# Nine buffers of prepared weights instead of five in a one-core hybrid decoder layer

## The reference

```python
a = rmsnorm(x, g_mix); u = a @ w_in                     # 1024 x 3080, w_in
# mLSTM heads from q, k, v, gates (chunkwise), short convolution from three more column groups
x = x + jnp.concatenate([h_m, y_c], axis=-1) @ w_out    # 1024 x 1024
f = rmsnorm(x, g_ffn)
x = x + (jax.nn.silu(f @ w_gate) * (f @ w_up)) @ w_down # width 2816
e = rmsnorm(pe @ w_ple, g_ple)                          # pe: 256 wide
x = x + jax.nn.sigmoid(x @ w_pg) * e                    # 1024 x 1024
y = rmsnorm(x, g_final)
```

## Time and profile before

| | |
|---|---|
| median of three runs | 2605.38 us |
| the profiled execution | 2609.61 us, its span 2607.6 us |
| PE busy | 2484.1 us (95%) |
| PEld busy | 2420.1 us (93%) |
| DVE / ACT / POOL busy | 1490.1 / 905.3 / 1014.5 us |
| DMA | 501.02 MB, 192 GB/s |
| granted TensorE clock | 0.983 of full speed |

### The profile page before, as it was taken

How to read it: one execution, slowest core, us unless ns; L and a number is a source line. 1 busy time by engine, 2 the same in 40 slices (tenths; PEclk the granted TensorE clock), 3 DMA queues, 4 the chain that set the end, 5 groups by cost and what they waited for, 6 DMA issues and landing times.

```text
span 2607.6 us, 41062 instructions
## 1 busy us (share of the span) xinstructions
PE 2484.1 (95%) x15829; PEld 2420.1 (93%) x15829; DVE 1490.1 (57%) x2307; ACT 905.3 (35%) x1688; POOL 1014.5 (39%) x785
## 2 busy tenths in 40 slices
PE   8898888999999999999999999999999999999997
PEld 7888778999999998999999999998899999999997
DVE  7667887655555684476643333468357664332355
ACT  5343443343334442334322121354134431211233
POOL 5555655576666242222232122333222232322233
PEclk8999999999999999999999999999999999999999
DMA  6556635576566746575556545575667555564545
GB/s 195 209 174 224 224 133 187 182 274 226 202 227 232 226 148 207 162 243 178 192 169 202 170 148 176 178 231 170 191 181 244 180 187 174 189 211 156 174 140 170
DMA packets 285044, 501.02 MB, mean 192 GB/s; under 512 B 18427, under 2 KB 182612, under 8 KB 284342
## 3 DMA queue, kind: packets, MB, share of 16 engines
q1 hardware_dynamic: 212182, 273.59, 31.1%
q10 hardware_dynamic: 72672, 224.82, 26.4%
HBM read 374.70 MB, written 123.65 MB: 191 GB/s over the span
## 4 chain that ended last, share of the span: by engine, by line
PE 74%; DVE 7%; DMA 3%; issue 3%; POOL 2%; ACT 1%; DVEq 0%; ACTq 0%; POOLq 0%; SPq 0%
PE bank L606 24%; PE bank L608 23%; PE bank L607 23%; DMA wring<-weight_parts 2%; POOL wring L2692 1%; DVE qlo L1798 1%; DMA xs<-x_prompt 1%; PE bank L730 1%; DVE ess L2415 1%; PE bank L797 1%; PE bank L741 1%; DMA wraw<-w_gate 0%; PE bank L719 0%; PE bank L803 0%; DVE wraw L1788 0%
## 5 line engine op out<-in xcount | busy, mean ns | idle before, releaser
L2692 POOL TENSOR_TENSOR wring<-wraw,wring 128x512 fp32r<-128x512 f32 x531 | 775.4, 1468 | 1250.1 <-ACT wring L1295 1247.9
L606 PE MATMUL bank<-qhi,wring 128*128 128x352 f32 (+1 forms) x3588 | 1173.2, 327 | 71.9 <-DVE u L1909 14.5
L608 PE MATMUL bank<-qhi,wring 128*128 128x352 f32 (+1 forms) x3588 | 1157.1, 322 | 0.0
L607 PE MATMUL bank<-qlo,wring 128*128 128x352 f32 (+1 forms) x3588 | 1155.5, 322 | 0.0
L606 PEld LDWEIGHTS bank<-qhi,wring 128*128 128x128 f32 x3588 | 684.0, 191 | 95.3 <-issue 85.1
L607 PEld LDWEIGHTS bank<-qlo,wring 128*128 128x128 f32 x3588 | 683.6, 191 | 0.0
L608 PEld LDWEIGHTS bank<-qhi,wring 128*128 128x128 f32 x3588 | 681.3, 190 | 0.0
L1295 ACT ACTIVATE wring<-wraw 128x512 fp32r<-128x512 f32 x531 | 331.0, 628 | 720.0 <-PE bank L608 549.2
L606 PE MATMUL bank<-hid,wring 128*128 128x352 f32 (+1 forms) x1056 | 340.6, 323 | 13.0 <-DVE wide L2498 7.5
L608 PE MATMUL bank<-hid,wring 128*128 128x352 f32 (+1 forms) x1056 | 339.0, 321 | 0.0
L607 PE MATMUL bank<-hid,wring 128*128 128x352 f32 (+1 forms) x1056 | 338.4, 320 | 0.0
(11 more groups left out here) (317 smaller groups left out, 2361.9 us busy)
## 6 DMA issues: line engine op xcount, KB each, us to landing
wring<-weight_parts ACTq DMA_DIRECT2D x418, 512.0 KB, 4.6
weight_parts<-wring SPq DMA_DIRECT2D x201, 512.0 KB, 4.0
wraw<-w_down SPq DMA_DIRECT2D x33, 1024.0 KB, 6.9
wraw<-w_in SPq DMA_DIRECT2D x14, 1024.0 KB, 6.5
wraw<-w_gate SPq DMA_DIRECT2D x11, 1024.0 KB, 6.0
wraw<-w_up SPq DMA_DIRECT2D x11, 1024.0 KB, 5.9
wraw<-w_in SPq DMA_DIRECT2D x44, 256.0 KB, 5.3
wraw<-w_gate SPq DMA_DIRECT2D x44, 256.0 KB, 4.1
```

What stands on the lines that cost most here:

```text
L606: nc.tensor.matmul(o, hi, mh, start=begins, stop=False, skip_group_check=True)
L607: nc.tensor.matmul(o, hi, ml, start=False, stop=False, skip_group_check=True)
L608: return nc.tensor.matmul(o, lo, mh, start=False, stop=ends, skip_group_check=True)
L2692: nc.gpsimd.tensor_tensor(wlo[e % RING][:, :].rearrange(v, k=k), w.src, whi[e % RING][:, :].rearrange(v, k=k), ALU.subtract).then_inc(lo_d ...
```

## The change

The ring gets nine buffers. The first five stay where they were, the other four lie at the upper end of the core's memory. The room comes from `dynamic_dma_scratch_size=512`: memory that is set aside by default for DMAs issued by POOL is not set aside here, and everything else moves down by as much. The semaphores that count stores and loads of entries are ten of each instead of six.

The start is as before (DVE takes the turns of the first `NEAR` = 5 entries there). In super 0, behind products 49, 56, 63 and 70 of the stage in (the first product of in 7, 8, 9 and 10), each of DVE, ACT and POOL calls `ahead()` once more. From then on ACT and POOL make entry n+8 at product n, DVE the sum of entry n+9, to the end of the program. ACT waits for the entry nine places back.

```diff
-RING = 5
-AHEAD = 4
+PARTS = 10
+RING = 9
+NEAR = 5
+LOOK_FURTHER = (49, 56, 63, 70)
...
-    spare_raw = at("spare_raw", [P, 2048], F32, w0 + 20480 + RING * 4096 + 5632)
+    spare_raw = at("spare_raw", [P, 2048], F32, w0 + 20480 + NEAR * 4096 + 5632)
...
-    wring = [at(f"wring{p}", [P, 1024], F32R, w0 + 20480 + p * 4096) for p in range(RING)]
+    far = nc.sbuf_usable_end // 32 * 32 - (RING - NEAR) * 4096
+    wring = [at(f"wring{p}", [P, 1024], F32R, w0 + 20480 + p * 4096 if p < NEAR else far + (p - NEAR) * 4096)
+             for p in range(RING)]
...
-    mix0 = w0 + 20480 + RING * 4096
+    mix0 = w0 + 20480 + NEAR * 4096
...
-                    before = entries[e - RING].kept
-                    if before:
-                        act.wait_ge(parts_kept[before % 6], 16 * ((before + 5) // 6))
+                    before = entries[e - RING].kept
+                    if before:
+                        act.wait_ge(parts_kept[before % PARTS], 16 * ((before + PARTS - 1) // PARTS))
...
             def in_after(q):
                 def after(s):
+                    if not q.n and s in LOOK_FURTHER:
+                        ahead()
...
-            for e in range(AHEAD + 1):
+            for e in range(NEAR):
                 ahead()
...
-    nc = bacc.Bacc("TRN2", target_bir_lowering=False, num_devices=1)
+    nc = bacc.Bacc("TRN2", target_bir_lowering=False, num_devices=1, dynamic_dma_scratch_size=512)
```

More of the change, by code:

```diff
@@ L287, in build @@
     y_roots = keep("y_roots", [P, 3])
-    assert cursor[0] <= nc.sbuf_usable_end, (cursor[0], nc.sbuf_usable_end)
+    assert cursor[0] <= far, (cursor[0], far)
     y_end = [at(f"y_end{p}", [P, D], F32, R0 + p * 4096) for p in range(3)]
@@ L513, in build @@
         landed = [sem("landed_even"), sem("landed_odd")]
-        parts_kept, parts_loaded = [sem(f"parts_kept{j}") for j in range(6)], [sem(f"parts_loaded{j}") for j in range(6)]
+        parts_kept, parts_loaded = [sem(f"parts_kept{j}") for j in range(PARTS)], [sem(f"parts_loaded{j}") for j in range(PARTS)]
         sums, hi_done, lo_done, prod = sem("sums"), sem("hi_done"), sem("lo_done"), sem("prod")
@@ L595, in entry_ready @@
                 else:
-                    pe.wait_ge(parts_loaded[w.loads % 6], 16 * ((w.loads + 5) // 6))
+                    pe.wait_ge(parts_loaded[w.loads % PARTS], 16 * ((w.loads + PARTS - 1) // PARTS))
             def operand_ready(q, st, i):
@@ L1089, in keep_parts @@
                         sp.dma_start(weight_parts[w.kept - 1], wring[e % RING][:, :].bitcast(F32))\
-                            .then_inc(parts_kept[w.kept % 6], 16)
+                            .then_inc(parts_kept[w.kept % PARTS], 16)
             def spare_weights(i):
@@ L1283, in one_ahead @@
                     if before:
-                        act.wait_ge(parts_kept[before % 6], 16 * ((before + 5) // 6))
+                        act.wait_ge(parts_kept[before % PARTS], 16 * ((before + PARTS - 1) // PARTS))
                 if w.loaded:
-                    act.wait_ge(parts_kept[w.loaded % 6], 16 * ((w.loaded + 5) // 6))
+                    act.wait_ge(parts_kept[w.loaded % PARTS], 16 * ((w.loaded + PARTS - 1) // PARTS))
                     act.dma_start(wring[e % RING][:, :].bitcast(F32), weight_parts[w.loaded - 1])\
-                        .then_inc(parts_loaded[w.loads % 6], 16)
+                        .then_inc(parts_loaded[w.loads % PARTS], 16)
                     return
```

## The result

The changed kernel is slower: 2622.48 us (median of four runs, 2619.66 to 2624.28) against 2605.12 us for the kernel before beside it, a ratio of 1.0065 (95% interval 1.005 to 1.008). A second timing gave 2622.62 against 2606.02 us, 1.0062 (1.0045 to 1.0079). The profiled execution took 2622.72 us, its span is 2620.7 us: 13.1 us more than the span before. The traces so show 13.1 of the 17.4 us between the medians, since the execution profiled before the change lay 4.2 us above its median.

What follows compares the result with a forecast made beforehand. The prediction saw gains only at PE's idle times, mostly waits for DVE's P6 evictions; -6 -4 +0 +1 +1 = -8 took 2609.6 to 2601.6 us profiled, 2597.4 as a median, called 2597.5, range 2585 to 2611.

Steps and rivals of the forecast that it cites:

- (a): Supers 1 and 2: PEld's 8.1 us of waits for loads can go; ends -8.1 and -2, taken as -6 us.
- (b): Gate and up, super 0: sums moved ahead of `hid` and P6 evictions shorten PE's waits; ends -8 and +2, taken -4 us.
- (c): Duo of out, super 0: first raw-load bubble's gain is offset by a second and DVE's longer list; -8 to +5, taken 0.
- (d): In 7 to in 10, super 0: each extra turn costs DVE at most one sum; ends 0 and +5, taken +1 us.
- The exchange named beside it: ACT no longer waits for the store of the entry five back; worth 0 to -3 us to PE, taken with (b).
- (f): Memory, semaphores and SP's list: no instruction added and the memory taken has no user, 0.
- (e): Pg, supers 0 and 1: ACT waits for pg 2's raw load, delaying PE; -1 to +6 per super, +1 together.
- The signs I had named for a wrong forecast: ACT's wait at pg 2 beyond 8 us, or PE's two waits in out together changing by more than 8 us.
- The rule weighed: DVE and POOL exclude each other in SBUF: super 0's sums meet POOL more often, PE +8, 2605.5 us; chance 0.06.
- Slower by the raw load in pg: Rival: ACT stands before a raw load SP can't issue earlier, 6 us in each of two supers, about 2610 us; chance 0.16.

Runs made afterwards that it cites:

- ring_only: The changed kernel with its nine buffers and ten semaphores but no extra turns, splits four entries ahead as in the kernel before: 2594.76 us, ratio 0.9963.

## Why the prediction was wrong

I forecast 2597.5 us, in 2585 to 2611, gave slower 0.16, and measured 2622.48. On the scale of the profiled execution the forecast was 2601.6 and the time is 2622.7 us. By the steps of the prediction, with the change in stall from before to after:

*(a) Waits for loads, supers 1 and 2: -6.* The mechanism was right, the loads' waits went. But supers 1 and 2 without their pg stall 3.2 us less than before, where ring_only, which keeps three waits for loads, has 7.5 us less. The turns bought those waits off and paid more elsewhere, 3.3 us of it in the stage in of super 2 (66.5 us of stall in ring_only, 69.8 after).

*(b) Sums moved in gate and up of super 0: -4, with ends at -8 and +2.* This step failed; it is the one term that came out beyond its ends. Gate 1 gained what I said (3.9 us, and nothing of it in ring_only). Gate 5 gained 4.2 us, but 3.3 of them come with the buffers alone, with S4 still in front of the eviction, so the reason I gave there, that S4 goes, is worth 0.9 us at most. And I took the two places where PE waited before as all that could change, and did not ask where the sums go in the pairs that were free of waits. Behind the up pairs S4, S1 and S2, 4.2 us in the rows above, arrived ahead of the hidden blocks, and the hidden blocks met POOL. Measured: 5.0 us more stall in gate and up than before, 6.6 more than in ring_only.

*(c) The duo of out: 0, with +5 as the upper end.* Out and ple stall 4.3 us more, near that end. Of the two bubbles I weighed the exchange was near even, 16.1 us of PE's waits before and 14.1 after; the loss is a third one that I did not have, the raw load of up 0 in front of out 3's evictions, 4.96 us.

*(d) The four extra turns: +1.* In stalls +1.0 us, but 3.2 us against ring_only; both are inside the ends of 0 and +5. The exchange named beside it, ACT free of the kept stores, worth 0 to -3, was too small together with *(f) memory: 0*: the buffers without turns are worth 10 us. It is not what put the forecast too low. What I did not see is that the turns cost 28 us from there.

*(e) The raw load in pg: +1, with ends at -1 and +6 per super.* This is the second term that was mis-sized. Step by step it went as I said: ACT stood there as early, relative to PE the load landed when I said (some 9 us of lateness are brought in), ACT waited 6.15 us, PE 3.30. The cost was +2.1 us in super 0 and +5.7 in super 1. In super 0 PE's later wait for tile 4, 2.33 us, did go, as I had counted; but I used super 0's row for both, and in super 1 PE's wait there was only 1.0 us. Against ring_only, where PE has no such wait, the two pg cost 13.1 us.

Added up: -3.2, +5.0, +4.3, +1.0 and +7.8 are +14.9 where I had -8, and down gave back 1.0. Most of the miss is (b), 9 us, and (e), 7 us. The signs I had named for a wrong forecast did not show it: ACT's wait stayed under 8 us, and PE's two waits in out changed by 2 us.

*The rule weighed.* The case made of it, 40 us more of DVE and 2605.5 us, did not come: DVE's busy time is 1490.1 us before, 1488.5 after and 1485.1 in ring_only. DVE and POOL do slow each other, but not more often: of DVE's instructions with two operands some 210 take over 0.2 us more than the shortest of their kind, before (211) and after (209). What changed is which instructions are hit, and those on which PE waits were among them.

*The rivals.* "Slower by the raw load in pg" named a true mechanism. Its price, +12, is near the 13.1 us that the two pg cost against ring_only; against the kernel before it is 7.8 of the 13.8 us, and there it was one of three. Its 2610 us was still too low. All three have one form, an instruction of an in-order list moved ahead of an eviction.

## What to carry to other kernels

A deeper buffer ring does two separate things: it frees the engine that fills it from the one that empties it and from the stores of what it holds, and it allows the fill to stand earlier in an in-order list. Try the first alone; here it gave 10 us, and the second took up to 28 back. How far ahead something is prepared had no direction here, where the list has a period of seven products: each step rearranges what stands in front of every eviction and what runs beside it, so it must be read at all places of the period, those without a wait above all. And one pair of traces is good for a total, not for a stage: between two traces of the same kernel single stages differed by up to 2.7 us.

## What was not expected of the hardware

The same DVE multiplication of a hidden block took 0.88 us in an idle time of POOL and 1.93 us beside it, an operand's low part 1.86 and 4.02 us. With DVE's total busy time within 0.3% of each other in ring_only and the changed kernel (1485.1 and 1488.5 us), their times differ by 1.1%: what matters of this contention is which instruction it hits.
